# Two quarters of the expert gathers go tile by tile, and one ranking is spread over 25 steps

## The reference, cut to what matters

```python
sc = jnp.einsum('thpd,hpnd->thpn', qr, subkeys)          # 4 heads x 2 x 128 scores a token
s1, i1 = lax.top_k(sc[:, :, 0], 16); s2, i2 = lax.top_k(sc[:, :, 1], 16)
best, flat = lax.top_k(s1[..., :, None] + s2[..., None, :] (as 256), 16)
experts = e1 * 128 + e2          # 64 rows a token;  gates = softmax(best)
hid = einsum('cd,ced->ce', x, take(u, experts))          # 64 dots a token
out = einsum('ce,ced->cd', gates * gelu(hid), take(v, experts))
```

## Time and profile before

| | us |
|---|---|
| median of 3 runs | 2737.16 (2736.84 to 2739.09) |
| profiled execution | 2735.84 |
| its span, first to last instruction | 2733.9 |
| quarter 0, first gather to first gather of quarter 1 | 313.4 to 733.7 |
| quarter 3, first gather to end of its sums | 1523.6 to 1962.5 |

### The profile page before, as it was taken

The page is one execution under the profiler, slowest core; times in us unless marked ns, Lnnn a source line. Parts: engine busy times, 40 slices in busy tenths (PEclk is TensorE's granted clock), DMA queues, the critical chain, the costliest instruction groups (busy, mean ns, idle before and its releaser), DMA issues.

```text
span 2733.9 us, 36972 instructions
## 1 busy us (share of the span) xinstructions
PE 1998.7 (73%) x14519; PEld 1244.9 (46%) x14519; DVE 1475.6 (54%) x3358; ACT 487.4 (18%) x816; POOL 1195.9 (44%) x1389
## 2 busy tenths in 40 slices
PE   5989576688486865688946388738598878778763
PEld 3666463445054451355523166423287545444431
DVE  3777899743884286763563696892146232212213
ACT  2203211021111410104311101210113111111101
POOL 2111356666665766765755655775500012212212
PEclk9999898899697986899978699869799989989976
DMA  9996699999999999999999989999854568999996
GB/s 345 347 342 228 247 332 406 409 389 368 409 396 409 409 406 408 398 409 396 382 390 354 357 322 365 368 406 386 339 180 123 203 264 347 406 427 409 415 428 276
DMA packets 239703, 970.70 MB, mean 355 GB/s; under 512 B 28029, under 2 KB 30181, under 8 KB 227271
## 3 DMA queue, kind: packets, MB, share of 16 engines
q0 software_dynamic: 193696, 696.80, 66.1%
q1 hardware_dynamic: 39568, 265.32, 24.1%
q10 hardware_dynamic: 6296, 6.57, 0.7%
HBM read 951.92 MB, written 16.68 MB: 354 GB/s over the span
## 4 chain that ended last, share of the span: by engine, by line
DMA 31%; PE 29%; DVE 16%; POOL 13%; issue 8%; ACT 3%; SPq 1%; POOLq 0%; DVEq 0%; ACTq 0%
POOL arena L465 12%; DMA arena<-in_peer_v_dram,arena 10%; PE psum L212 10%; DMA y_slots<-arena 8%; DVE arena L477 6%; PE psum L802 6%; DMA arena<-in_w_up_dram 4%; PE psum L572 4%; DMA arena<-in_peer_u_dram,arena 4%; PE psum L815 2%; DMA arena<-in_ada_w_dram 1%; PE psum L2547 1%; DVE arena L678 1%; DMA arena<-in_w_in_dram 1%; DMA arena<-in_hgrn_w_in_dram 1%
## 5 line engine op out<-in xcount | busy, mean ns | idle before, releaser
L477 DVE CUSTOM_DVE_ANT_0 arena<-arena,psum 128x1024 f32<-128x1024 f32 x512 | 596.0, 1216 | 108.4 <-DMA arena<-in_peer_u_dram,arena 107.1
L465 POOL DMA_INDIRECT arena<-in_peer_v_dram,arena x512 | 501.2, 979 | 302.3 <-PE psum L572 141.5
L465 POOL DMA_INDIRECT arena<-in_peer_u_dram,arena x512 | 493.4, 964 | 278.7 <-issue 138.0
L572 PE MATMUL psum<-arena 128*32 128x512 f32 x2048 | 314.8, 744 | 235.6 <-DMA arena<-in_peer_v_dram,arena 232.4
L212 PE MATMUL psum<-arena 128*128 128x256 f32 (+3 forms) x1664 | 387.1, 394 | 66.9 <-DVE arena L2097 16.7
L802 PE MATMUL psum<-arena 128*128 128x256 f32 x1664 | 382.7, 392 | 37.8 <-DMA arena<-in_sb_w_q_dram 12.9
L802 PEld LDWEIGHTS psum<-arena 128*128 128x128 f32 x1664 | 324.8, 197 | 99.8 <-issue 18.2
L212 PEld LDWEIGHTS psum<-arena 128*128 128x128 f32 x1664 | 296.1, 198 | 160.7 <-issue 57.7
L2622 POOL DMA_DIRECT2D y_slots<-arena x188 | 93.4, 497 | 398.2 <-DVE arena L2608 373.9
L572 PEld LDWEIGHTS psum<-arena 128*32 128x32 f32 x2048 | 68.1, 124 | 427.8 <-issue 414.2
L2547 PE MATMUL psum<-arena 128*32 128x256 f32 x3008 | 197.5, 421 | 64.4 <-DMA arena<-in_w_up_dram 52.4
(11 more groups left out here) (390 smaller groups left out, 2067.0 us busy)
## 6 DMA issues: line engine op xcount, KB each, us to landing
arena<-in_w_gate_dram SPq DMA_DIRECT2D x32, 2048.0 KB, 19.1
arena<-in_w_up_dram SPq DMA_DIRECT2D x32, 2048.0 KB, 23.6
arena<-in_w_down_dram SPq DMA_DIRECT2D x32, 2048.0 KB, 16.4
arena<-in_ada_w_dram POOLq DMA_DIRECT2D x20, 2048.0 KB, 11.7
arena<-in_hgrn_w_in_dram SPq DMA_DIRECT2D x10, 2048.0 KB, 11.8
arena<-in_kv_w_dram POOLq DMA_DIRECT2D x8, 2048.0 KB, 13.7
arena<-in_w_in_dram POOLq DMA_DIRECT2D x7, 2048.0 KB, 12.2
arena<-in_w_in_dram SPq DMA_DIRECT2D x7, 2048.0 KB, 8.0
```

Of the source, the lines that this page charges most:

```text
L465: pool.indirect_dma_start(RING(n, k), None, (U_TAB, V_TAB)[v], bass.IndirectOffsetOnAxis(ap=at, axis=0))\
L477: last = dve.tensor_tensor_reduce(out=row, in0=row, in1=bank(XB0, 0, D), scale=1.0, scalar=0.0, op0=ALU.mult, op1=ALU.add, accum_out=par_s ...
L572: last = pe.matmul(bank(ACC + half, 0, 512, parts=(32 * g, 32)), lhsT=mem("t", D + (s // 4 % 2) * 512 + (g * GR + s % 4) * 32, 32), rhs=RI ...
```

## The change

Quarters 0 and 3 take the order 16 dots of a, 16 sums of a, 16 dots of b, 16 sums of b. The steps of turning, gelu, gates, finishing and spreading move accordingly, `turn_rows_pe` of the second tile waits for the first tile's finish, and in these two quarters the turned weights are copied at the same step in which PE turns them. The ranking of the second tile (tile 1 in quarter 0, tile 7 in quarter 3) has its ten slices at steps 1, 3, 5, 7, 9, 12, 14, 16, 18 and 20, where before they were at 1, 1, 2, 3, 4, 5, 6, 7, 8 and 9. Segments of blocks and loads of weights keep their steps.

```diff
-        ORDERS = [sums_first if w else order(8) for w in range(TILES // 2)]
+        in_turn = [(v, b, s) for b in range(2) for v in range(2) for s in range(NS)]
+        IN_TURN = lambda w: w in (0, 3)
+        ORDERS = [in_turn if IN_TURN(w) else sums_first for w in range(TILES // 2)]
...
             pe.wait_ge(sem("experts"), t + 1)
-            if t >= 2:
+            if IN_TURN(t // 2) and t % 2:
+                pe.wait_ge(sem("acc_used"), t)
+            elif t >= 2:
                 pe.wait_ge(sem("acc_used"), t - t % 2)
...
-        ROUTES = ({(0, 1): (1, 0.9), (2, 6): (55, 0.5), (3, 7): (1, 0.9)}
+        ROUTES = ({(0, 1): (1, 2.2), (2, 6): (55, 0.5), (3, 7): (1, 2.2)}
...
-        ROWS_AT, TURN_AT = lambda w: (2, 16 if w in (0, 3) else 3), lambda w: (18, 46) if w else (21, 44)
+        ROWS_AT, TURN_AT = lambda w: (2, 36 if IN_TURN(w) else 3), lambda w: (16, 48) if IN_TURN(w) else (18, 46)
+        FINISH_AT = lambda w: 35 if IN_TURN(w) else 3 * NS
         SLICES = 12
-        SPREADS = [{SUM_AT(w, 0) if w else 23: (0, (0, 1)), SUM_AT(w, 3) + 1: (0, (2,)), SUM_AT(w, 8) + 1: (0, (3,)),
-                    47 if w else 46: (1, (0,)), 49: (1, (1,)), 53: (1, (2,)), 57: (1, (3,))} for w in range(TILES // 2)]
+        SPREADS = [{SUM_AT(w, 0): (0, (0, 1)), SUM_AT(w, 3) + 1: (0, (2,)), SUM_AT(w, 8) + 1: (0, (3,)),
+                    48 if IN_TURN(w) else 47: (1, (0,)), 49: (1, (1,)), 53: (1, (2,)), 57: (1, (3,))} for w in range(TILES // 2)]
...
-                    if s == 14:
+                    if s == (30 if IN_TURN(w) else 14):
                         gate_exp_act(act, b)
-                    if s == (16 if w else 18):
+                    if s == (15 if IN_TURN(w) else 16):
                         gelu_act(act, a)
-                    if s == (45 if w else 41):
+                    if s == (47 if IN_TURN(w) else 45):
                         gelu_act(act, b)
...
-                    if s - 1 in TURN_AT(w):
-                        turn_dve(dve, a + TURN_AT(w).index(s - 1))
-                    if s == 3 * NS:
+                    turned_at = s if IN_TURN(w) else s - 1
+                    if turned_at in TURN_AT(w):
+                        turn_dve(dve, a + TURN_AT(w).index(turned_at))
+                    if s == FINISH_AT(w):
                         finish_dve(dve, a, link)
```

## The result

| | us |
|---|---|
| changed kernel, median of 20 runs | 2736.04 |
| kernel before on the same chip, median of 20 runs | 2742.22 |
| ratio after to before, 95% interval | 0.9977 [0.9967, 0.9987], so 6.2 us less |
| forecast | 12.6 us less |

The sign was right, half of the gain is missing. So spans are no use for a verdict; ratios of medians are used for that, and profiles for where time goes inside an execution.

A forecast was written before the change was run, and what follows sets the result against it. The gather chain, POOL to ring to user, was taken to set quarters 0 and 3. Terms +1 and -13.5 sum to -12.5 us: 2723.3 against the profiled 2735.8, 2724.6 as median; range 2716 to 2733.

The forecast's parts named there:

- Quarter 3, -13.5 us: Quarter 3: b's sums start at 1856 instead of 1869.47, so 13.5 us gained; bounds -30 to +3 us.
- Its first reason: Quarter 3, dots of a: three ranking slices (12 us) leave DVE, taken as 9 us; dots end at 1646.5, before 1655.5.
- The further steps of the forecast: Quarter 3: a's first sum at 1651 (before 1685.92), sums and gates alternating at 9.1 us, b's first dots 9.8 us earlier.
- Quarter 0, +1 us: Quarter 0: b's sums start 6.5 us later, 5.5 us of transfer regained, so it ends 1 us later; bounds -10 to +12.
- its last sentence: Quarter 0, sums of b: the old order lost 5.5 us of transfer from 645 to 681, which the new one does not.
- The sums on DVE and PE (97 us and 58 us): Quarter 0: DVE has 97 us of work in b's dots; PE has 58 us in six projections and eight sums of a.
- Rival A: Quarters 0 and 3 both fill up with transfers, -8 and -19 us: 2710 us; chance 0.20.
- Rival B: Quarter 0: b's dots bind on DVE, b's sums over 13 us late, quarter 3 gives under 5: +8, 2745; chance 0.18.
- C: Transfers are hidden anyway: each quarter's first-half win is lost in its second half, change 0, 2737 us; chance 0.12.
- D: PE's clock: cold starts after sums-free dots stretches cost 24 us at worst, half on the path: 2737 us; chance 0.05.

## Why the prediction was half right

*Quarter 3, -13.5 us: right in size by the medians* (15 and 14 measured), *less clearly by the stamps.* Its first reason was 9 us in the dots of a from the slices taken out of them. The reason holds; the stamps give 2 to 8 us for it in four profiles, and about 7 between the paces in the new order. The first sum of a comes 29 to 35 us earlier (35 forecast), the first of b 6 to 15 us earlier and not 13.5 in each profile. A part of the gap to the medians lies in which executions were profiled: both of the kernel before lie 5 to 6 us below its medians, the four with the change 1 to 6 us above theirs. The further steps of the forecast (first sums of a early, gates and sums alternating) are where the order by itself would have shown, and at the old pace it gives 3 us, which its interval does not tell from nothing. The forecast never separated the two, and so could not say that one line of the change, the pace, carries it.

*Quarter 0, +1 us: this is the step that failed.* Up to b's first sum it holds to a microsecond: 652 against a forecast of 651. What failed is its last sentence, "5.5 us of transfer lost, which the new order, with the same bytes left, does not lose". That term was to be 5.5 us and measured nothing: from b's first sum to quarter 1's first gather it takes 89.2 to 90.6 us in the six profiles with the old order and 90.6, 88.9 and 90.3 with the new one, 90 in the mean of either. From 614 to 674 the old order leaves 6 to 9 us of transfer idle and the new one 6, 3 and 4. The lull behind b's first sum is still there; I read it as the ring standing full through the handover and then PE's projections beside the first sums, but no run took these away. So the 6.5 us by which b's sums start late remain: the quarter takes 426.7 us as the mean of the three profiles with the changed quarter 0, 6.4 more than the mean of the six with the old one, and costs 8.5 us by the medians. That is 7.5 us more than forecast; quarter 3 gave 1 to 2 us more than its 13.5, and together this is the 6.4 us by which the change fell short.

The sums on DVE and PE (97 us and 58 us) that the forecast used were right: from b's first dot to the end of its last it takes 97 to 98 us, and from a's first sum to that of step 24 59. The experiments support both as bounds in the new order, DVE more clearly than PE. What it did not ask is what transfers did in these stretches before: 403 and 406 GB/s in one profile, 405 and 393 in the other. Stretches that are nearly full have little to win and much to lose.

*Rivals.* Rival A (both fill) is out. Rival B named the place and the price in quarter 0, b's dots against 97 us of DVE work and up to +12; but neither of its conditions came: b's sums start 6 to 7 us late and not 13, and quarter 3 gives more than 5. C (gained in front, lost behind) describes quarter 0, not the kernel. D is out as a price of the handovers: PE's first sums after three of the four took 1.92 us, at full clock, and only the one at 440.35 took 3.49. The clock does cost time elsewhere, as the next paragraph shows.

*A chance of the execution.* In the three profiles with quarter 0 alone changed and 47 blocks of expert rows, what follows quarter 2 takes 1218 to 1220 us, against 1210 and 1212 in the two of the kernel before, though the code there is the same. Of this, 3 to 7 us lie in one place, b's sums of quarter 3: they take 96 to 97 us in these three, 93 and 90 in the two before. The same difference stands between the two profiles of the changed kernel, 90.3 and 95.4 us, and there the clock goes with it. Here are 19 us around the eighth sum of b, and one group of the block's products in them, first in the profile of 90.3, then in that of 95.4:
```profile
1917.50:1936.50 19.00, 12.86 (x80) 5.56 (x80) 3.40 (x7) 2.88 (x6) 10.32 (x12) 0.73 1.03 407
...
1924.67 3.93 PE L212 MATMUL psum<-arena 128*128 128x36 f32 x32
...
1912.80:1931.80 19.00, 15.42 (x72) 8.78 (x76) 2.44 (x6) 2.89 (x6) 7.49 (x8) 0.50 0.98 388
...
1919.95 7.04 PE L212 MATMUL psum<-arena 128*128 128x36 f32 x32
```
The granted clock is 0.50, the 1.2 GHz level, all through the second. Of the 17 profiles ten have this group at 3.9 to 4.4 us and b's sums at 90 to 93, seven at 7.0 us and 95 to 97. One kernel can show either, so the difference need not come from quarter 0; whether some kernels draw the slow one more often is not shown.

*Left open.* Of the 8.5 us that quarter 0 costs by the medians, about 6.4 are traced to quarter 0, which is within the interval of the 8.5 (5 to 12). Nor is it shown that no other placing of segments would pay, or what the pace gives in the old order.

## What to carry to other kernels

Before a reorder, ask of each stretch not only which engine would be full after it, but whether the shared resource (here the transfers) is full there now: a stretch at its ceiling has nothing to win and can only lose, and relieving an engine in a stretch gives back there at most the time for which the resource stood idle. Two engines that were each loaded by a different kind of step are both covered when the steps are mixed; put in turn, each can become the bound once. An experiment that leaves work out changes the numbers, so look whether what depends on them later, here the count of expert blocks, is still the same. And where a change has two parts, price them apart: here a pace of one ranking gave more than the whole change, and one of the two quarters took half of it away again.

## What the runs showed of the hardware

Executions of the two kernels spread by 12 and 16 us here (2726.7 to 2742.5 for the changed one), and the profiled ones are drawn from that spread, so that two single profiles differed by 6 us with the wrong sign. A part of it goes with the clock: the five fastest of the changed kernel's 20 runs had a mean granted clock of 0.868 to 0.874, the five slowest 0.862 to 0.866. The length of quarter 0 stayed within 2.3 us over six profiles with its old order, but lay 4.6 us apart in two profiles of the changed kernel. The four 0.5 MB gathers of a step moved 408 to 410 GB/s from 494 to 534 us in each of the 17 profiles, with PE and DVE loaded differently in them, and relieving either engine did not lift the rate above that.
